# The level products of a chunked recurrence as full 128x128 tiles, with the Gram products in blocks of their own

## What is computed

```python
def step(s, inp):
    r_t, w_t, k_t, v_t, a_t, b_t = inp
    sa = jnp.einsum('bhvk,bhk->bhv', s, a_t)
    s = s * w_t[:, :, None, :] + sa[..., None] * b_t[:, :, None, :] + v_t[..., None] * k_t[:, :, None, :]
    y = jnp.einsum('bhvk,bhk->bhv', s, r_t) if emit else None
    return s, y
```

## Time and profile before

| what | value |
|---|---|
| median of 3 runs | 2888.08 us (2887.6 to 2889.34) |
| profiled execution, its span | 2891.8 us |
| TensorE busy | 2785.9 us of the span |
| VectorE, ScalarE busy | 1191.4 us, 685.4 us |
| MATMUL records, each with a LDWEIGHTS record | 29030 |

### The profile page before, as it was taken

How to read it: one execution, slowest core, us unless ns; L and a number is a source line. 1 busy time by engine, 2 the same in 40 slices (tenths; PEclk the granted TensorE clock), 3 DMA queues, 4 the chain that set the end, 5 groups by cost and what they waited for, 6 DMA issues and landing times.

```text
span 2891.8 us, 63838 instructions
## 1 busy us (share of the span) xinstructions
PE 2785.9 (96%) x29030; PEld 1672.3 (58%) x29030; DVE 1191.4 (41%) x2524; ACT 685.4 (24%) x1425; POOL 3.0 (0%) x7
## 2 busy tenths in 40 slices
PE   7999999999999999999998999989999999999997
PEld 4467777445777888864577787863333333333332
DVE  4777565444546444237786564431111011011101
ACT  2345312544322111013454126520000000000000
POOL 0000000000000000000000000000000000000000
PEclk9999999999999999999999999999999999999999
DMA  7100143212232433232000442459999999999995
GB/s 293 59 3 4 47 148 122 66 44 84 91 127 78 146 117 90 80 120 84 30 4 5 168 160 96 148 218 348 413 364 365 415 359 378 400 364 412 364 379 199
DMA packets 188786, 534.55 MB, mean 185 GB/s; under 512 B 6112, under 2 KB 80096, under 8 KB 171104
## 3 DMA queue, kind: packets, MB, share of 16 engines
q1 hardware_dynamic: 187440, 526.21, 48.5%
q0 software_dynamic: 1072, 4.19, 0.4%
HBM read 528.29 MB, written 2.10 MB: 183 GB/s over the span
## 4 chain that ended last, share of the span: by engine, by line
PE 92%; DVE 3%; ACT 2%; issue 1%; SPq 1%; DMA 0%; DVEq 0%; ACTq 0%
PE bank L583 68%; PE bank L711 12%; PE bank L1357 8%; PE bank L829 2%; PE bank L1219 1%; SPq L3014 1%; ACT WR L1647 1%; DMA rep<-in_repeated 0%; ACT ar L1647 0%; PE bank L948 0%; DVE WR L2480 0%; DVE RS L2351 0%; PE bank L1519 0%; DVE ar L2410 0%; ACT L1647 0%
## 5 line engine op out<-in xcount | busy, mean ns | idle before, releaser
L583 PE MATMUL bank<-AT,WR 128*128 128x512 f32 (+1 forms) x1408 | 519.9, 519 | 6.3 <-ACT AT L1647 3.7
L1647 ACT ACTIVATE ar<-bank 128x256 f32<-128x256 f32 (+2 forms) x338 | 155.1, 463 | 1533.4 <-PE bank L583 1026.5
L583 PE MATMUL bank<-WR,ar 128*32 128x512 f32 (+1 forms) x4464 | 444.5, 555 | 1.6 <-DVE ar L2923 1.6
L583 PE MATMUL bank<-ar 128*32 128x512 f32 (+6 forms) x3990 | 429.6, 509 | 9.7 <-ACT ar L1647 5.7
L583 PEld LDWEIGHTS bank<-AT,WR 128*128 128x128 f32 x1408 | 262.4, 191 | 212.5 <-issue 196.4
L583 PEld LDWEIGHTS bank<-ar 128*32 128x32 f32 (+3 forms) x3990 | 176.1, 124 | 248.3 <-issue 236.4
L583 PEld LDWEIGHTS bank<-WR,ar 128*32 128x32 f32 x4464 | 143.7, 110 | 288.4 <-issue 285.8
L1647 ACT ACTIVATE WR<-bank 128x512 f32<-128x512 f32 (+1 forms) x224 | 125.1, 593 | 200.2 <-PE bank L583 166.7
L583 PE MATMUL bank<-AT,ar 128*32 128x512 f32 (+1 forms) x1456 | 151.4, 561 | 11.9 <-ACT AT L1647 11.9
L2933 DVE TENSOR_TENSOR YB<-YB,bank 128x512 f32<-128x512 f32 x28 | 18.0, 684 | 343.3 <-PE bank L583 343.3
L2941 DVE TENSOR_TENSOR ar<-ar,bank 128x512 f32<-128x512 f32 (+1 forms) x48 | 29.8, 621 | 286.5 <-PE bank L583 285.1
(11 more groups left out here) (368 smaller groups left out, 3296.6 us busy)
## 6 DMA issues: line engine op xcount, KB each, us to landing
WR<-in_moe_w_down SPq DMA_DIRECT2D x27, 2048.0 KB, 15.2
WR<-in_ada_w SPq DMA_DIRECT2D x20, 2048.0 KB, 8.2
ar<-in_moe_w_down SPq DMA_DIRECT2D x20, 2048.0 KB, 14.7
WR<-in_w_in SPq DMA_DIRECT2D x18, 2048.0 KB, 8.9
WR<-in_moe_w_gate SPq DMA_DIRECT2D x18, 2048.0 KB, 17.0
WR<-in_moe_w_up SPq DMA_DIRECT2D x15, 2048.0 KB, 16.2
WR<-in_moe_w_up SPq DMA_DIRECT2D x18, 1536.0 KB, 7.8
WR<-in_moe_w_gate SPq DMA_DIRECT2D x15, 1536.0 KB, 9.1
```

Source lines behind the costliest of these rows:

```text
L583: return pe.matmul(o, lhsT, rhs, start=first, stop=last)
L1647: return act.activation(out, in_, func, **k)
```

## The change

The strict parts of the two heads of a pair are put into one 128x128 tile LB[:, q, :], each as a 64x64 block off the diagonal (rows of h, columns of 1 - h), the rest zero. A level is then 8 products of the full tile with 64 moving columns of X, where it was 16 products of 64x64 tiles. The Gram product LT is written with h and 1 - h exchanged, and T1 is exchanged for n = 0 as it was for the other levels. Nothing stands beside a level any more: the values follow level 2 as a block of 16 products, and the new gram_ahead issues X behind level 3 and LT behind level 4. LB is a single tile for all steps, where LT had two. begin_turned is now three predicated copies (two of 64 partitions into LB, one into XT); the fill of the tiles before the loop changes with it.

```diff
-    masks.append(two(lambda d: (r // 2 == c // 2) & later[d](c, r) | (r == c)))
+    masks.append(two(lambda d: (r // 2 == c // 2) & later[d](c, r)))
...
-        LTs = [HTf[:, 3072 + 512 * b:3584 + 512 * b] for b in range(2)]
+        LB = HTf[:, 3072:4096].rearrange("p (q w) -> p q w", q=8)
...
                 def gram(i, what, bank, q, h):
                     ba, aa = BK[i % 2][64 * h:64 * h + 64, q, 0:64], pair(MV[:, i % 2, 0, :], q, h)
-                    return mm(pair(bank, q, h), *((aa, ba) if what == "X" else (ba, aa)), True, True)
-
-                def level(i, n, beside=None):
+                    if what == "X":
+                        return mm(pair(bank, q, h), aa, ba, True, True)
+                    return mm(pair(bank, q, 1 - h), ba, aa, True, True)
+
+                def gram_ahead(i, what):
+                    if what == "X":
+                        pe.wait_ge(operands_ready, seen(operands_ready))
+                        pe.wait_ge(A.free, A.jobs[("vt", l, i - 1, 1)])
+                    else:
+                        pe.wait_ge(S.free, S.jobs[("gram", l, i, "X")])
+                    for q, h in hq:
+                        last = gram(i, what, gram_bank, q, h)
+                    last.then_inc(S.full, 1)
+                    S.done(("gram", l, i, what))
+
+                def level(i, n):
                     if n:
                         pe.wait_ge(A.free, A.jobs[("X", l, i, n - 1)])
                     else:
-                        pe.wait_ge(inverse_ready, seen(inverse_ready))
+                        pe.wait_ge(inverse_ready, seen(inverse_ready, 2))
                         if i:
                             pe.wait_ge(A.free, A.jobs[("G", l, i - 1)])
...
                     for q in range(8):
                         bank = level_banks(i, n)[q // 4]
-                        for h in range(2):
-                            ins = mm(pair(bank, q, 1 - h if n else h), pair(LTs[i % 2], q, h), pair(X[n > 0], q, h), True, True)
+                        ins = mm(bank[:, 64 * q:64 * q + 64], LB[:, q, :], X[n > 0][:, 64 * q:64 * q + 64], True, True)
                         if q % 4 == 3:
                             ins.then_inc(S.full, 1)
                             S.done(("T1", l, i, n, q // 4))
-                        for h in range(2 if beside else 0):
-                            if beside == "solve":
-                                solve(i - 1, q, h)
-                            elif beside == "values":
-                                value_turned(i, q, h)
-                            else:
-                                last = gram(i + 1, beside, gram_bank, q, h)
...
-                        level(i, 2, "values")
+                        level(i, 2)
+                        for q, h in hq:
+                            value_turned(i, q, h)
...
-                    level(i, 3, "X" if i < NCH - 1 else None)
+                    level(i, 3)
+                    if i < NCH - 1:
+                        gram_ahead(i + 1, "X")
                     against(i, 4)
                     inverse_doubled(i, 3)
                     against(i, 6)
-                    level(i, 4, "LT" if i < NCH - 1 else None)
+                    level(i, 4)
+                    if i < NCH - 1:
+                        gram_ahead(i + 1, "LT")
...
                 def begin_turned(i, bank=banks[7]):
 
-                    LT = LTs[i % 2]
-                    dve.copy_predicated(dq(LT), mk(M_STRICT_T).bitcast(u32), step_product(bank)).then_inc(S.free, 1)
-                    dve.wait_ge(S.free, S.taken)
-                    v(TT(dq(XT[0]), dq(LT), mk(M_PAIR_T), ALU.mult), inverse_ready, wait=False)
+                    S.take()
+                    dve.wait_ge(S.full, S.taken)
+                    for h in range(2):
+                        rows, turned = slice(64 * h, 64 * h + 64), slice(64 - 64 * h, 128 - 64 * h)
+                        ins = dve.copy_predicated(dq3(LB[rows, :, turned]), mk(M_STRICT_T)[turned].bitcast(u32), dq(bank)[turned])
+                        ins.then_inc(inverse_ready, 1)
+                    dve.copy_predicated(dq(XT[0]), mk(M_PAIR_T).bitcast(u32), dq(bank)).then_inc(S.free, 1)
...
-                for x in (X[0], LTs[0], LTs[1]):
+                v(dve.tensor_copy(LB, swap.unsqueeze(1).to_broadcast([128, 8, 128])), wait=False)
+                for x in (X[0], XT[0]):
                     v(dve.tensor_copy(x, eyes), wait=False)
```

More of the change, by code:

```diff
@@ L831, in narrow @@
                 return last
-            def compact(x):
-                return lambda q, h: pair(x, q, h)
             def swapped(x):
@@ L895, in level @@
                             S.done(("T1", l, i, n, q // 4))
-                        for h in range(2 if beside else 0):
-                            if beside == "solve":
-                                solve(i - 1, q, h)
-                            elif beside == "values":
-                                value_turned(i, q, h)
-                            else:
-                                last = gram(i + 1, beside, gram_bank, q, h)
-                    if beside in ("X", "LT"):
-                        last.then_inc(S.full, 1)
-                        S.done(("gram", l, i + 1, beside))
                 def inverse_doubled(i, n):
-                    x, t1 = (swapped(XT[1]), swapped(T1)) if n else (compact(XT[0]), compact(T1))
+                    x, t1 = swapped(XT[n > 0]), swapped(T1)
                     if n:
@@ L2447, in dq, with dq3 @@
                     return x.rearrange("p (d q w) -> p d q w", d=2, q=4)
+                def dq3(x):
+                    return x.rearrange("p (d q) w -> p d q w", d=2)
                 def mk(m):
```

## The result

The changed kernel takes 2970.83 us (median of 4 runs, 2969.76 to 2971.12) against 2888.24 us before: 1.0278 times as long, 95% interval 1.0263 to 1.0292. The profiled execution spans 2968.8 us, 77.0 us more than the 2891.8 before. By the medians it is 82.6 us: a run's span is some 1.8 us shorter than its time, so the execution that was profiled before is about 5 us longer than the median one.

The account below looks back on a forecast made before the run. TensorE's work in program order, with a sixth of idle time in it, was taken to bound the kernel. 70 + 39 + 6 - 28 = +87 us on the median of 2888.08 gave 2975 us, range 2940 to 3008.

Parts of the forecast that it names:

- (e): Idle time in both recurrences, behind issue, ScalarE and VectorE, takes in part of the added work: -28 us, bounds 0 and -52.
- (a): 80 levels of the recurrences: 8 full-tile products, paced by the 128-column load, replace 16 small ones; +70 us.
- (b): 42 blocks of Gram and value products that shared the levels' time now take their own; +39 us.
- (c): Changes of tile shape between TensorE runs in the recurrences: about 60 more at 0.1 us each, +6 us.
- (d): VectorE in begin_turned and the fills: three predicated copies are covered by other work, costed at nothing; 12 us without cover.
- R1: Levels: 64 moving columns pace a full-tile product at 0.029 us a record; -20 us, 2868 us; chance 6%.
- R2: Levels: pace 0.058 us a record, idle time takes in the Gram blocks; -7 to +17 us, 2881 to 2905; 6%.
- R3: Recurrences: idle time takes nothing in, since instruction-queue stalls stay and new waits replace old; +115 us, 3003 us; 10%.
- R4: Recurrences: the granted clock falls to a mean of 0.9, adding 53 us; 3028 us; chance 7%.
- Its other sign: Fewer than 270 MATMUL records in a 10 us slice were expected; otherwise the stalls of the instruction queue stay.
- The reading of "issue": TensorE's issue waits in the recurrences are instructions arriving too slowly, at some 33 records a microsecond.

Follow-up runs that it names:

- e3_small: Changed kernel with each level as 16 products of 64x64 tiles, Gram blocks still by themselves; 2897.75 us, ratio 1.0018 to the kernel before.
- e9_wide: Changed kernel with 128 moving columns instead of 64 in six of eight full-tile level products; 2970.56 us.
- e2_halves: Changed kernel with each full-tile level product issued as two products of 128 rows and 64 columns; 2905.73 us, ratio 1.0051 to the kernel before.
- e1_blocks: Kernel before with the 42 Gram and value blocks issued behind their level, levels left as 16 products of 64x64 tiles; 2898.19 us, ratio 1.0016.
- e5_beside: Changed kernel with values and Gram products interleaved again with full-tile level products, two small ones behind each; 3110.59 us, ratio 1.0755 to the kernel before.
- e6_spare: Kernel before with 16 unread products more beside level 1 of steps 1 to 7, in idle tiles; 2906.58 us, ratio 1.0044.
- e7_spare_after: Changed kernel with 832 records more of unread products beside value and Gram X blocks, in idle tiles; 2970.36 us, ratio 1.0272 to the kernel before.
- e8_no_values: Kernel before without 14 of the 16 turned-value products beside level 2 in steps 1 to 7; 2887.78 us, ratio 0.9979.

## Why the prediction was right, point by point

**Sum and sign.** 2975 us forecast, 2970.8 measured; +87 us, of which 82.6 came on the medians and 77 on the spans. Some of this closeness is luck: the work added came out 3 us larger than forecast, and what the idle time took in 7 to 13 us larger, see (e). The added time lies in the two recurrences, as it had to: from the first to the last begin_inverse 32.7 us in layer 0 (169.1 before, 201.8 after), 34.5 us in layer 1 (165.3, 199.8), and the other 10 us after the last begin_inverse of each layer, where its last step lies.

**(a) Level products, +70 us.** Right: 0.113 us a record was taken, 0.115 is in the rows, and taking the full tile out again gave 75 us (e3_small). That the load and not the moved columns set it, which was argued from tiles with 3 and 8 moving columns, is borne out by e9_wide and e2_halves together: neither the moved columns nor the number of products changed the pace as the width of the tile did. The 81 ns that the Trainium skill (TensorE: Matmul & The Clock Gate, "Back-to-back issue gap") gives is not what f32 tiles do here: 115 ns.

**(b) Blocks, +39 us.** Right as time on the array: each block of 32 records is 1.08 us from the start of one piece to the next in the timeline, the change of shape behind it included. As a price it depends on the rest: alone they cost 5 us (e1_blocks). The changed kernel is dear because the full tiles use up the same idle time. The sum had this right only because idle time was taken off once for all terms.

**(c) Changes of shape, +6 us.** Right in kind. 0.1 us between long runs (1.93 us from a level's start to the next piece, of which 16 x 0.115 = 1.84 are its records); between runs of one and two products 0.14 (e5_beside). The forecast left that out of e5_beside's expectation, and it is a part of what was off there.

**(d) VectorE, nothing.** Right within the noise: e3_small and e1_blocks agree within 1 us, with intervals of 3, and VectorE waits 1.85 us behind the copies.

**(e) Idle time taken in, -28 us.** The step that was mis-sized. By the rows of after, levels add 80 x 0.91 = 73 us, blocks 39 and shapes 6, 118 in all, and the spans grew by 77: 41 us were taken in, or 35 by the medians. By source: "issue" fell from 21 us to 2.5 (0.4 and 0.9% of 190 us), where 16 were taken off; VectorE from 10 to about 5 (0 and 2.3%), where 6 were; ScalarE stood at 22 us as before, where I had taken off 6: the waits of 0.40 and 0.68 us are all still there. That is 24 in the rows of the chain, and TensorE's idle time over the whole span says the same: 105.9 us before (2891.8 less 2785.9), 82.5 after. The other 17 us stood as busy time before: TensorE's busy time grew by 100.4 us and not by 118. The blocks account for them, since in e1_blocks, which has the blocks and nothing else, busy time grew by 22 us for 39. About half is found: a stall hides its first 0.2 us behind the last product's own time (the record before the stall of 0.69 us in the earlier trace rows starts at 273.35, the next at 274.26, 0.91 us later), and with 41 stalls in the two recurrences, short ones included, that is 8 us. The rest stays open.

**The rivals.** R1 and R2 (a pace of 0.029 or 0.058) fell with the rows at 0.115. R3 (stalls stay) fell with "issue" at 0.4 and 0.9% and no stall of over 0.1 us in either stretch. Its other sign did not hold everywhere: most slices of 10 us have fewer than 270 MATMUL records (216 between 280 and 290 us), but that from 210 to 220 has 309, and without a stall. R4 (the clock falls) did not happen in the changed kernel, but it is real: e5_beside has it, with a mean of 0.90 between 200 and 370 us.

**The reading of "issue".** It was an inference from a flat rate and two stalls; e6_spare and e7_spare_after show it: the same unread products cost 13 us in one kernel and nothing in the other. The packets of the instruction queue, which the prediction did not lay beside the stalls, show it in the trace of before already.

## What to carry to other kernels

Count a change of tile shape in loaded columns for each tile that can take turns, not in products: two 64-column tiles in turn load as many columns as one full tile in half the time, and four tiles in turn hide whole blocks. Before paying array time for fewer instructions, look whether the stalls named "issue" end at a fixed distance behind the packets of the instruction queue, and test it by adding unread products in idle tiles. And before counting on idle time, take it off once for all terms, since two edits that each fit into it don't fit together.

## What the runs showed of the hardware

- Products of full 128*128 f32 tiles start every 0.115 us a record with 64 and with 128 moving columns alike (e9_wide), while 128*64 tiles (e2_halves) and 64*64 tiles in turn start every 0.029 us with 64.
- TensorE's instructions come at some 33 records a microsecond over long stretches (5183 to 5290 in 160 us in the kernel before, e1_blocks and e6_spare, whatever their products were), about 64 bytes for each load or matmul record. The packets of 16384 bytes start every 3.8 to 3.9 us there. Beyond that the trace shows stalls named "issue", up to 1.7 us long, in the middle of runs that wait for nothing; in the stretches read, 33 of 33 before and 54 of 54 in e6_spare end 1.2 to 1.6 us after a packet's end.
- Leaving out 392 records gave back 6 us, where 12 would be their share at 33 a microsecond (e8_no_values); why only half is not shown.
- The granted clock fell to a mean of 0.90 between 200 and 370 us with TensorE busy for nearly 99% of the time, where a full-tile product and two small ones alternate (e5_beside). In the six microseconds from 310 to 316, ahead of one of the falls to 0.50 (1.2 GHz), the engine had not stood idle. The changed kernel, with the same products in blocks, kept 1.00 (2.4 GHz) in every slice of 10 us from 150 to 380 and from 1450 to 1680 us.
